# Heads stage of a hybrid decoder trunk: one more place for finished and for unfinished units, weights of a group in two transfers, their splits spread, attention's first loads moved

## Chip, cores and metric

One core of a Trainium2 chip runs the whole program. Times are device microseconds (us) of one execution, lower is better. The engines are called PE (TensorE; PEld is its weight load), DVE (VectorE), ACT (ScalarE), POOL (GpSimd) and SP (SyncE, here only the issuer of transfers).

## What is computed

Two decoder layers on 1024 tokens of width 1024 in float32. Layer 0 is a pooling and a short-convolution mixer, layer 1 is multi-head latent attention with 16 heads. The change lies in layer 1, between its input projection and its attention:

```python
q = (rms_norm(c_q, q_lat_g) @ w_uq).reshape(B, S, MLA_HEADS, QK_HEAD)
kv = (rms_norm(c_kv, kv_lat_g) @ w_ukv).reshape(B, S, MLA_HEADS, QK_NOPE + V_HEAD)
k_nope, v = kv[..., :QK_NOPE], kv[..., QK_NOPE:]
k = jnp.concatenate(
    [k_nope, jnp.broadcast_to(k_rope[:, :, None, :], (B, S, MLA_HEADS, QK_ROPE))], axis=-1)
q = rope_tail(rms_norm(q, q_head_g), cos, sin)
k = rope_tail(rms_norm(k, k_head_g), cos, sin)
o = causal_attention(q, k, v)
```

The latents have 768 (query) and 256 (key-value) columns, a head 64 plain and 32 rotated columns, and 64 columns of values.

## The kernel before

`front` computes layer 0 and the latents of layer 1 (up to 567 us of the span), `heads_and_attention` the heads and the attention, `final_projection` the rest. The change is in `heads_and_attention`, and in `Joint`, which holds what the first two share.

**Units.** The heads stage works on 32 units: 4 groups of 4 heads (g), each over 8 tiles of 128 tokens (t); u = 8 g + t. For exactness each float32 product is three matmuls, high x high, high x low, low x high (`three_passes`, L104 to L108), so each operand exists as a high half, rounded by ACT, and a low half, the rest, subtracted by DVE. A unit is on PE two chunks of the key-value weights (6 matmuls of 512 columns) and then six of the query weights (18 of 384).

**The way of a unit.** After PE, in step u:
- ACT copies v to its place (four places, `VSLOTS`), k and q to a place of `x` (seven, `XSLOTS`, L1340, L1346), and squares them (L1343, L1347).
- DVE sums the squares (L1448, L1452). After every fourth unit it takes the inverse roots for those four in a chain of 12 small operations (`root`, L1381 to L94). Then it scales unit u - 3 (L1405, L1406).
- POOL finishes a scaled unit: rotation and gain (`finish`, L1141 to L1506), and raises `turned`.
- ACT writes the high half of unit u - 5 to a place of `y` (two places, `head_split`, L1303). It waits for `turned` and for the store of the unit that had the place before, u - 7.
- DVE subtracts for the low half (L1410), and SP stores the place to `qk_scratch` in memory (L1236).

A step's waits and work stand in this order on each engine, and an engine does nothing past a wait that isn't met. PE may run about two units ahead: unit u needs the squares of unit u - 2, which need DVE's sums of unit u - 4.

**Weights of the next group.** While a group runs, the next one's weights are loaded (SP, `load_group`, at its first unit, for groups 2 and 3), and split by ACT (high, L1294) and DVE (low, L1375) in steps t = 3 to 6, by the table `when`. PE waits in the first unit of a group for each chunk (`w_done`). The raw weights of even and odd groups have one place each; even low halves lie where their raw ones were.

**Into attention.** SP reads keys and queries of a head back transposed (`load_k`, L1240, and `load_q`, L1243), and values of two heads at once (`load_v`, L1246). Their places (`k_t`, `q_t`) lie on space that the heads stage has left. The last units are finished inside attention: from unit 28 on by POOL alone, and their stores stand among attention's loads. In step 31 PE first computes the scores of the first two tiles of head 0, then unit 31. In attention, step n computes scores of tile n + 2, so head 1 (tile 8) is first used in step 6.

```python
            act.wait_ge(turned, w + 1)
            if w >= 2:
                act.wait_ge(y_stored[w % 2], 16 * (w // 2))
...
            if t == 0 and 1 <= g < G - 1:
                load_group(g + 1)
...
            store_v(u)
            if split_in(u) >= 0:
                store_qk(split_in(u))
```

SP has one queue, in program order: `load_group`, `store_v(u)`, `store_qk(u - 5)`, and, in some steps, the loads for attention ahead of them.

Of the kernel before, what the change touches and what calls it, by code (L numbers as in the profile page):

```python
# [142 lines left out]
class Joint:  # L143


    def __init__(self, nc, ctx, ring_at, w_place, lat_lo):
# [17 lines left out]
        self.kv_lo0, self.uq_lo0 = [kv_lo[:, k, :] for k in range(KKV)], [uq_lo[:, k, :] for k in range(KQ)]  # L164
        kv_hi = at("kv_hi0", [P, KKV, KVG], F32R, ring_at + tile)
# [843 lines left out]
def heads_and_attention(nc, w_ukv, w_uq, arena2, ring_at, w_place, banks_ps, joint, rms_qkv, rms_v, q_tab, k_rope, k_rope_ss,  # L1009
# [5 lines left out]
    XSLOTS, VSLOTS, LAG = 7, 4, 2  # L1015
# [24 lines left out]
    x = after("x", [P, XSLOTS, 2, HPG, QKH])  # L1040
    y = after("y", [P, 2, 2, HPG, BLK], F16)
# [18 lines left out]
    k_t = [at("k_t0", [P, 2, S], F16, ring_at), at("k_t1", [P, 2, S], F16, ring_at + TILE)]  # L1060
    q_t = [at("q_t0", [P, 2, S], F16, ring_at + 3 * TILE), at("q_t1", [P, 2, S], F16, ring_at + 2 * TILE)]
# [16 lines left out]
    w_landed = sem("w_landed")  # L1078
# [6 lines left out]
    y_stored = [sem(f"y_stored{e}") for e in range(2)]  # L1085
# [29 lines left out]
    when = {3: chunks[0:1], 4: chunks[1:3], 5: chunks[3:5], 6: chunks[5:8]}  # L1115
# [94 lines left out]
    def sync(sp):  # L1210
        def load_group(g):
# [17 lines left out]
        def store_qk(w):  # L1229
# [25 lines left out]
        for u in range(UNITS):  # L1255
# [35 lines left out]
    def scalar(act):  # L1291
        def weight_high(g, chunk):
            act.wait_ge(w_landed, 16 * NCH * g)
# [36 lines left out]
        for u in range(UNITS):  # L1330
# [9 lines left out]
            nc.scalar.activation(x[:, u % XSLOTS, 1, :, :NOPE], kv_view(u)[:, :, :NOPE], ACT.Copy, scale=rms_kv)  # L1340
# [5 lines left out]
            nc.scalar.activation(x[:, u % XSLOTS, 0], q_view(u), ACT.Copy, scale=rms_q)  # L1346
# [23 lines left out]
    def vector(dve):  # L1370
# [32 lines left out]
        def scale(w):  # L1403
            q, k = x[:, w % XSLOTS, 0], x[:, w % XSLOTS, 1, :, :NOPE]
# [359 lines left out]
```

## Time and profile before

| | us |
|---|---|
| median of 3 runs | 1048.66 (1046.89 to 1048.79) |
| the profiled execution, its own time | 1049.41 |
| span of its profile | 1047.4 |
| PE busy | 1017.0 (97%) |
| DVE busy | 616.3 (59%) |
| ACT busy | 465.0 (44%) |
| POOL busy | 211.1 (20%) |
| mean granted clock of PE over the span | 0.989 of full |

The profile is of one execution. Start times count from the span's start; a row of the timeline gives start, duration, engine, line of the kernel, operation, out<-in, shapes, and in brackets how long the engine was idle before it and what ended that. A wait for several things is put down to the one whose last event came last by the profile; where the engine named had long been done, it was another, often a transfer. A busy share is a mean over stages: the heads stage runs from 567 to 722 us, attention follows.

### The profile page before, as it was taken

How to read it: one execution, taken by the hardware profiler on the slowest of the kernel's cores; microseconds unless marked ns; L12 is line 12 of the kernel's file. 1: busy time of each engine (PE TensorE's matmuls, PEld its weight loads, DVE VectorE, ACT ScalarE, POOL GpSimd, SP SyncE). 2: the span in 40 equal slices, each digit the busy share in tenths (PEclk: the TensorE clock that was granted, in tenths of full speed). 3: DMA queues.
4: the chain of work that ended last, by engine and by line, in shares of the span. 5: the costliest groups of instructions: out<-in, count | busy, mean ns of one | idle time of the engine just before them, and what ended most of it. 6: DMA issues, size and time to landing. Idle time of an engine off the chain costs nothing. (4 is left out here: it accounts for less than half of the span.)

```text
span 1047.4 us, 15498 instructions
## 1 busy us (share of the span) xinstructions
PE 1017.0 (97%) x5979; PEld 846.2 (81%) x5979; DVE 616.3 (59%) x1111; ACT 465.0 (44%) x868; POOL 211.1 (20%) x301
## 2 busy tenths in 40 slices
PE   6999999999999999999999999999999999997998
PEld 4888888888888888888888998987777777775887
DVE  5653554445644543311344679798999999996221
ACT  6301111111132322322144657667999999997000
POOL 0000000000000001200001366786663332321000
PEclk9999999999999999999899999999999999998999
DMA  9300211211333431412112053664686564521221
GB/s 281 51 25 21 61 41 41 61 41 41 121 100 128 154 141 41 126 41 54 28 41 76 26 202 114 220 201 145 134 203 155 120 138 108 95 42 61 101 91 70
DMA packets 166425, 103.10 MB, mean 98 GB/s; under 512 B 76496, under 2 KB 150736, under 8 KB 166096
## 3 DMA queue, kind: packets, MB, share of 16 engines
q1 hardware_dynamic: 159280, 101.73, 34.4%
q10 hardware_dynamic: 7072, 0.39, 0.5%
q8 instruction: 47, 0.77, 0.3%
q14 instruction: 26, 0.21, 0.1%
HBM read 55.96 MB, written 29.36 MB: 81 GB/s over the span
## 5 line engine op out<-in xcount | busy, mean ns | idle before, releaser
L106 PE MATMUL banks<-front_act_hi,front_w_hi 128*128 128x512 f32 x608 | 240.8, 396 | 10.0 <-DVE front_w_lo L525 10.0
L107 PE MATMUL banks<-front_act_lo,front_w_hi 128*128 128x512 f32 x608 | 238.5, 392 | 0.0
L108 PE MATMUL banks<-front_act_hi,front_w_lo 128*128 128x512 f32 x608 | 238.5, 392 | 0.0
L106 PEld LDWEIGHTS banks<-front_act_hi,front_w_hi 128*128 128x128 f32 x608 | 115.4, 190 | 35.8 <-issue 8.5
L107 PEld LDWEIGHTS banks<-front_act_lo,front_w_hi 128*128 128x128 f32 x608 | 115.6, 190 | 24.4 <-issue 0.5
L108 PEld LDWEIGHTS banks<-front_act_hi,front_w_lo 128*128 128x128 f32 x608 | 115.3, 190 | 24.3
L392 ACT ACTIVATE front_w_hi<-front_w 128x1024 fp32r<-128x1024 f32 x43 | 45.6, 1060 | 147.2 <-DMA front_w<-in_w_in_ab 102.8
L1427 DVE TENSOR_TENSOR heads_pt_lo<-banks,heads_pt_hi 128x512 f16<-128x512 f32 (+2 forms) x192 | 102.1, 554 | 11.3 <-ACT heads_pt_hi L1318 6.7
L374 POOL TENSOR_TENSOR front_sq<-front_sq,front_squares 128x1024 f32<-128x1024 f32 x6 | 14.4, 2396 | 450.3 <-ACT front_squares L487 450.3
L1318 ACT ACTIVATE heads_pt_hi<-banks 128x512 f16<-128x512 f32 (+2 forms) x192 | 88.7, 486 | 10.3 <-PE banks L1586 10.2
L529 DVE TENSOR_TENSOR front_w_lo<-front_w,front_w_hi 128x1024 fp32r<-128x1024 f32 x43 | 52.3, 1219 | 42.8 <-ACT front_w_hi L392 42.6
L1604 PE MATMUL banks<-heads_v,heads_pt_hi 128*128 128x128 f16 x576 | 74.4, 220 | 0.9 <-DVE heads_pt_lo L1427 0.9
L1419 DVE CUSTOM_DVE_ANT_0 heads_probs_big<-banks,heads_mask,score_scale 128x1024 f32<-128x1024 f32 (+1 forms) x64 | 68.7, 1073 | 3.6 <-PE banks L108 2.6
L1586 PE MATMUL banks<-ident,heads_probs_big 128*128 128x128 f32 x416 | 69.0, 279 | 1.4 <-ACT heads_probs_big L1309 1.3
L1605 PE MATMUL banks<-heads_v,heads_pt_lo 128*128 128x64 f16 x576 | 69.4, 193 | 0.0
L1309 ACT ACTIVATE heads_probs_big<-heads_probs_big,heads_neg_max 128x1024 f32<-128x1024 f32 (+1 forms) x64 | 63.4, 991 | 5.5 <-DVE heads_neg_max L1419 3.3
L106 PE MATMUL banks<-heads_k_t,heads_q_t 96*128 96x512 f16 (+2 forms) x192 | 62.9, 328 | 1.8 <-DVE heads_neg_max L1419 1.8
L107 PE MATMUL banks<-heads_k_t,heads_q_t 96*128 96x512 f16 (+2 forms) x192 | 62.3, 324 | 0.0
L108 PE MATMUL banks<-heads_k_t,heads_q_t 96*128 96x512 f16 (+2 forms) x192 | 61.5, 325 | 0.0
L1604 PEld LDWEIGHTS banks<-heads_v,heads_pt_hi 128*128 128x128 f16 x576 | 54.0, 99 | 2.2 <-DVE heads_pt_lo L1427 1.0
L106 PE MATMUL out_proj<-gate_hi,w_out_hi 128*128 128x512 f32 x128 | 51.0, 398 | 2.7 <-DVE w_out_lo L961 2.6
L1605 PEld LDWEIGHTS banks<-heads_v,heads_pt_lo 128*128 128x128 f16 x576 | 51.3, 98 | 2.2
(246 smaller groups left out, 2067.7 us busy)
## 6 DMA issues: line engine op xcount, KB each, us to landing
qk_scratch<-heads_y SPq DMA_DIRECT2D x32, 512.0 KB, 3.7
front_w<-in_w_in_ab SPq DMA_DIRECT2D x21, 512.0 KB, 3.9
front_w<-in_w_in_c SPq DMA_DIRECT2D x17, 512.0 KB, 4.0
y<-in_x_t SPq DMA_DIRECT2D x8, 512.0 KB, 8.1
front_w<-in_w_out_ab SPq DMA_DIRECT2D x8, 512.0 KB, 3.8
front_x<-in_x_t SPq DMA_DIRECT2D x8, 512.0 KB, 5.1
x_scratch<-front_x SPq DMA_DIRECT2D x8, 512.0 KB, 4.0
v_scratch<-heads_v SPq DMA_DIRECT2D x32, 128.0 KB, 3.0
```

The source lines that it names most:

```text
L106: nc.tensor.matmul(out, w_hi, a_hi, start=first, stop=False)
L107: nc.tensor.matmul(out, w_hi, a_lo, start=False, stop=False)
L108: return nc.tensor.matmul(out, w_lo, a_hi, start=False, stop=last)
L392: nc.scalar.activation(weight(n, 1), weight(n, 0), ACT.Copy).then_inc(hi_done, 1)
L529: nc.vector.tensor_tensor(weight(n, 2), weight(n, 0), f32(weight(n, 1)), ALU.subtract).then_inc(lo_done, 1)
L1309: nc.scalar.activation(row, row, ACT.Exp, bias=neg_max[:, h % 2, i:i + 1], scale=-1.0, accum_out=total[:, h % 2, i:i + 1]).then_inc(exp_do ...
L1318: nc.scalar.activation(pt_hi[:, q % PIECES, :width], t_ps[:, banks[("piece", n, k)] % 3, :width], ACT.Copy).then_inc(pt_high, 1)
L1419: nc.vector.tensor_tensor_reduce(probs(n, 0, width), scores(i, 0, width), mask[:, S - width:], score_scale[:], 3e38, ALU.add, ALU.min, neg ...
L1427: nc.vector.tensor_tensor(pt_lo[:, q % PIECES, :width], t_ps[:, banks[("piece", n, k)] % 3, :width], pt_hi[:, q % PIECES, :width], ALU.sub ...
L1586: last = nc.tensor.transpose(t_ps[:, b, r * P:(r + 1) * P], probs(n, j * P, (j + 1) * P), ident[:])
L1604: nc.tensor.matmul(out, pt_hi[:, q % PIECES, blk], v2[e][:, j, :], start=(j == 0), stop=False)
L1605: last = nc.tensor.matmul(out[:, :VH], pt_lo[:, q % PIECES, blk], v2[e][:, j, :VH], start=False, stop=(j == i))
```

## The change

- `y` gets a third place and `x` an eighth. The new ones, `last_x` and `last_y`, lie on space of the first stage's weight ring. ACT's high half of unit w now waits for the store of unit w - 3.
- So the places of keys and queries move: `k_t0` and `q_t0` lie on the high weights of even groups, free when unit 23 is done; `k_t1` on their low query weights, free then too; `q_t1` on the high key-value weights of odd groups, free only when unit 31 is done on PE. Their loads move to later steps.
- `load_group` issues one transfer for the key-value weights and one for the query weights instead of two and six, with a semaphore for each.
- The table `when` spreads the eight splits over t = 2, 4, 5 and 6, two each.
- POOL clears `last_y` too.

```diff
@@ Joint @@
+        self.kv_raw_tile, self.uq_raw_tile = kv_raw, uq_raw
@@ heads_and_attention @@
-    XSLOTS, VSLOTS, LAG = 7, 4, 2
+    XSLOTS, YSLOTS, VSLOTS, LAG = 8, 3, 4, 2
...
-    x = after("x", [P, XSLOTS, 2, HPG, QKH])
-    y = after("y", [P, 2, 2, HPG, BLK], F16)
+    x, y = after("x", [P, XSLOTS - 1, 2, HPG, QKH]), after("y", [P, YSLOTS - 1, 2, HPG, BLK], F16)
+    last_x, last_y = at("last_x", [P, 2, HPG, QKH], F32, ring_at), at("last_y", [P, 2, HPG, BLK], F16, ring_at + 3 * TILE)
...
-    k_t = [at("k_t0", [P, 2, S], F16, ring_at), at("k_t1", [P, 2, S], F16, ring_at + TILE)]
-    q_t = [at("q_t0", [P, 2, S], F16, ring_at + 3 * TILE), at("q_t1", [P, 2, S], F16, ring_at + 2 * TILE)]
+    k_t = [at("k_t0", [P, 2, S], F16, ring_at + TILE), at("k_t1", [P, 2, S], F16, w_place + 2 * TILE)]
+    q_t = [at("q_t0", [P, 2, S], F16, ring_at + 2 * TILE), at("q_t1", [P, 2, S], F16, arena2)]
...
-    w_landed = sem("w_landed")
+    kv_landed, uq_landed = sem("kv_landed"), sem("uq_landed")
...
-    y_stored = [sem(f"y_stored{e}") for e in range(2)]
+    y_stored = [sem(f"y_stored{e}") for e in range(YSLOTS)]
...
-    when = {3: chunks[0:1], 4: chunks[1:3], 5: chunks[3:5], 6: chunks[5:8]}
+    when = {2: chunks[0:2], 4: chunks[2:4], 5: chunks[4:6], 6: chunks[6:8]}
...
+    def x_slot(w):
+
+        return last_x[:] if w % XSLOTS == XSLOTS - 1 else x[:, w % XSLOTS]
+
+    def y_slot(w):
+
+        return last_y[:] if w % YSLOTS == YSLOTS - 1 else y[:, w % YSLOTS]
...
@@ sync: load_group @@
-            for k in range(KKV):
-                sp.dma_start(kv_raw[g % 2][k], w_ukv[k * P:(k + 1) * P, g * KVG:(g + 1) * KVG]
-                             ).then_inc(w_landed, 16)
-            for k in range(KQ):
-                sp.dma_start(uq_raw[g % 2][k], w_uq[k * P:(k + 1) * P, g * QG:(g + 1) * QG]
-                             ).then_inc(w_landed, 16)
+            kv_tile, uq_tile = (kv_raw1, uq_raw1) if g % 2 else (joint.kv_raw_tile, joint.uq_raw_tile)
+            sp.dma_start(kv_tile[:], w_ukv.rearrange("(k p) c -> p k c", p=P)[:, :, g * KVG:(g + 1) * KVG]
+                         ).then_inc(kv_landed, 16)
+            sp.dma_start(uq_tile[:], w_uq.rearrange("(k p) c -> p k c", p=P)[:, :, g * QG:(g + 1) * QG]
+                         ).then_inc(uq_landed, 16)
...
@@ sync: the loop over units @@
-            if g == G - 2 and t == 4:
+            if g == G - 1 and t == 1:
                 group_stored(0)
+                sp.wait_ge(q_ready, (G - 1) * NT)
                 load_k(0)
-            if g == G - 2 and t == 6:
+            if g == G - 1 and t == 2:
                 load_q(0)
-            if g == G - 1 and t == 1:
-                sp.wait_ge(q_ready, (G - 1) * NT)
+            if g == G - 1 and t == 4:
                 load_k(1)
-            if g == G - 1 and t == 3:
-                load_q(1)
-            if g == G - 1 and t == 5:
+            if g == G - 1 and t == 6:
                 load_v(0)
             store_v(u)
+            if u == UNITS - 1:
+                sp.wait_ge(q_ready, UNITS)
+                load_q(1)
             if split_in(u) >= 0:
                 store_qk(split_in(u))
...
@@ scalar @@
-            act.wait_ge(w_landed, 16 * NCH * g)
+            act.wait_ge(kv_landed if chunk[0] == "kv" else uq_landed, 16 * g)
...
-            if w >= 2:
-                act.wait_ge(y_stored[w % 2], 16 * (w // 2))
+            if w >= YSLOTS:
+                act.wait_ge(y_stored[w % YSLOTS], 16 * (w // YSLOTS))
             else:
                 act.wait_ge(cleared, 1)
-            nc.scalar.activation(y[:, w % 2, :, :, :QKH], x[:, w % XSLOTS], ACT.Copy).then_inc(y_high, 1)
+            nc.scalar.activation(y_slot(w)[:, :, :, :QKH], x_slot(w), ACT.Copy).then_inc(y_high, 1)
...
@@ gpsimd @@
+        nc.gpsimd.memset(last_y[:].bitcast(F32), 0.0)
         nc.gpsimd.memset(y[:].bitcast(F32), 0.0).then_inc(cleared, 1)
```

Everywhere else `x[:, w % XSLOTS]` becomes `x_slot(w)` and `y[:, w % 2]` becomes `y_slot(w)`.

The order of instructions shows it at three places. The first is SP's queue at the start of group 2, where the third store of a unit stands ahead of the weights (`joint_kv_raw`, `joint_uq_raw`: the even group's raw weights). Before:

```order
L1236 DMA qk_scratch<-heads_y 256x1x1024
L1217 DMA joint_kv_raw_54<-in_w_ukv 128x512 x2
L1220 DMA joint_uq_raw_55<-in_w_uq 128x384 x6
L1226 DMA v_scratch<-heads_v 128x256
L1236 DMA qk_scratch<-heads_y 256x1x1024
```

and now:

```order
L1245 DMA qk_scratch<-heads_last_y 256x1x1024
L1227 DMA joint_kv_raw_54<-in_w_ukv 128x2x512
L1229 DMA joint_uq_raw_55<-in_w_uq 128x6x384
L1235 DMA v_scratch<-heads_v 128x256
L1245 DMA qk_scratch<-heads_y 256x1x1024
```

The eight issues between the stores of units 2 and 3 have become two.

The second is DVE in step 14, the last with splits of group 2's weights: sums, scaling, splits, low half of unit 9. Before:

```order
L1448 TENSOR_REDUCE heads_ss<-heads_sq 128x4
L1452 TENSOR_REDUCE heads_ss<-heads_sq 128x4
L1405 TENSOR_TENSOR heads_x<-heads_x,heads_rs 128x384
L1406 TENSOR_TENSOR heads_x<-heads_x,heads_rs 128x4x64
L1375 TENSOR_TENSOR joint_uq_lo_57<-joint_uq_raw_55,joint_uq_hi_1_60 128x384
L1375 TENSOR_TENSOR joint_uq_lo_57<-joint_uq_raw_55,joint_uq_hi_2_61 128x384 x2
L1410 TENSOR_TENSOR heads_y<-heads_x,heads_y 128x8x96
```

and now:

```order
L1458 TENSOR_REDUCE heads_ss<-heads_sq 128x4
L1462 TENSOR_REDUCE heads_ss<-heads_sq 128x4
L1415 TENSOR_TENSOR heads_x<-heads_x,heads_rs 128x384
L1416 TENSOR_TENSOR heads_x<-heads_x,heads_rs 128x4x64
L1385 TENSOR_TENSOR joint_uq_lo_57<-joint_uq_raw_55,joint_uq_hi_2_61 128x384 x2
L1420 TENSOR_TENSOR heads_y<-heads_x,heads_y 128x8x96
```

Two splits stand there instead of three; the first two of the group have moved from steps 11 and 12 to step 10.

The third is SP's queue at the end of the stage. Before, from the store ahead of step 27:

```order
L1236 DMA qk_scratch<-heads_y 256x1x1024
L1243 DMA_TRANSPOSE heads_q_t_125<-qk_scratch 128x2x1024
L1226 DMA v_scratch<-heads_v 128x256
L1236 DMA qk_scratch<-heads_y 256x1x1024
L1226 DMA v_scratch<-heads_v 128x256
```

and now, from the store of unit 25 ahead of step 31:

```order
L1245 DMA qk_scratch<-heads_y 256x1x1024
L1235 DMA v_scratch<-heads_v 128x256
L1252 DMA_TRANSPOSE heads_q_t_127<-qk_scratch 128x2x1024
L1245 DMA qk_scratch<-heads_last_y 256x1x1024
L1249 DMA_TRANSPOSE heads_k_t_124<-qk_scratch 128x2x1024
```

The queries of head 1 have moved from step 27 to behind everything but the store of unit 26; the keys of head 2 follow.

## Rows read from the trace of the kernel before

**Rows 1.** The page, part 1: busy time of the engines, share, instructions.
```profile
PE 1017.0 (97%) x5979; PEld 846.2 (81%) x5979; DVE 616.3 (59%) x1111; ACT 465.0 (44%) x868; POOL 211.1 (20%) x301
```

**Rows 2.** Timeline of PE: first matmuls of units and scores; start, duration.
```profile
567.43 0.39 PE L106 MATMUL banks<-joint_kv_hi,joint_lat_hi 128*128 128x512 f32 x1
...
639.88 0.39 PE L106 MATMUL banks<-joint_kv_hi,joint_lat_hi 128*128 128x512 f32 x1
...
644.90 0.55 PE L106 MATMUL banks<-joint_uq_hi,joint_lat_hi 128*128 128x384 f32 x1 [1.90 <-DVE joint_uq_lo L1375]
...
647.80 0.63 PE L106 MATMUL banks<-joint_kv_hi,joint_lat_hi 128*128 128x512 f32 x1
...
680.35 0.39 PE L106 MATMUL banks<-heads_kv_hi,joint_lat_hi 128*128 128x512 f32 x1
...
688.17 0.63 PE L106 MATMUL banks<-heads_kv_hi,joint_lat_hi 128*128 128x512 f32 x1
...
715.87 0.39 PE L106 MATMUL banks<-heads_k_t,heads_q_t 96*128 96x512 f16 x1
...
722.36 0.39 PE L106 MATMUL banks<-heads_k_t,heads_q_t 96*128 96x512 f16 x1
...
734.31 0.38 PE L106 MATMUL banks<-heads_k_t,heads_q_t 96*128 96x512 f16 x1 [0.69 <-DVE heads_neg_max L1419]
```

**Rows 3.** Windows, PE: stretch, length, busy, instructions, granted clock, DMA share, GB/s.
```profile
645.00:650.00 5.00, 5.00 (x18) 0.66 0.34 122
```

**Rows 4.** Timeline of DVE: first sums of units 8, 16, 24; waits; splits.
```profile
610.92 0.42 DVE L1448 TENSOR_REDUCE heads_ss<-heads_sq 128x4 f32<-128x256 f32 x1
...
625.10 0.96 DVE L1410 TENSOR_TENSOR heads_y<-heads_x,heads_y 128x768 f16<-128x768 f32 x1 [4.85 <-ACT heads_y L1303]
...
644.30 2.23 DVE L1375 TENSOR_TENSOR joint_uq_lo<-joint_uq_raw,joint_uq_hi 128x384 fp32r<-128x384 f32 x3
...
652.97 0.41 DVE L1448 TENSOR_REDUCE heads_ss<-heads_sq 128x4 f32<-128x256 f32 x1
...
665.57 1.20 DVE L1410 TENSOR_TENSOR heads_y<-heads_x,heads_y 128x768 f16<-128x768 f32 x1 [4.25 <-ACT heads_y L1303]
...
693.51 0.41 DVE L1448 TENSOR_REDUCE heads_ss<-heads_sq 128x4 f32<-128x256 f32 x1
```

**Rows 5.** Timeline of ACT: high half of unit 5.
```profile
624.22 0.84 ACT L1303 ACTIVATE heads_y<-heads_x 128x768 f16<-128x768 f32 x1 [5.90 <-POOLq L1507]
```

**Rows 6.** Timeline of POOL: last operation on unit 5.
```profile
617.87 0.46 POOL L1506 TENSOR_TENSOR heads_x<-heads_prod 128x128 f32<-128x128 f32 x1
```

**Rows 7.** Timeline of SP's queue: issues, start and duration.
```profile
611.66 1.48 SPq L1217 DMA_DIRECT2D joint_kv_raw<-in_w_ukv  x2
613.19 2.86 SPq L1220 DMA_DIRECT2D joint_uq_raw<-in_w_uq  x6
...
616.83 0.66 SPq L1236 DMA_DIRECT2D qk_scratch<-heads_y  x1
...
704.15 3.79 SPq L1243 DMA_TRANSPOSE heads_q_t<-qk_scratch  x1
...
724.67 0.72 SPq L1226 DMA_DIRECT2D v_scratch<-heads_v  x1
```

**Rows 8.** Issues from 616.5 to 617.4: count, KB, us to landing.
```profile
qk_scratch<-heads_y SPq DMA_DIRECT2D x1, 512.0 KB, 7.3
```

**Rows 9.** Issues from 611.5 to 616.05: the store of unit 2 among them.
```profile
joint_uq_raw<-in_w_uq SPq DMA_DIRECT2D x6, 192.0 KB, 4.8
qk_scratch<-heads_y SPq DMA_DIRECT2D x1, 512.0 KB, 3.7
```

**Rows 10.** Issues from 658.4 to 659: the store of unit 11.
```profile
qk_scratch<-heads_y SPq DMA_DIRECT2D x1, 512.0 KB, 5.9
```

**Rows 11.** The tile heads_y: durations in ns, least, median, most; first and last start.
```profile
L1410 DVE TENSOR_TENSOR heads_y<-heads_x,heads_y x27: 949/1211/1498, 599.0 to 730.8; 128x768 f16<-128x768 f32 x27
```

**Rows 12.** View of the transfers: all loads of a head's queries, median to landing.
```profile
heads_q_t<-qk_scratch SPq DMA_TRANSPOSE x16, 5.1
```

More of the change, by code:

```diff
@@ L1059, in heads_and_attention @@
     uq_lo = [joint.uq_lo0, chunks_of(at("uq_lo1", [P, KQ, QG], F32R, kv_at1 + half), KQ)]
-    k_t = [at("k_t0", [P, 2, S], F16, ring_at), at("k_t1", [P, 2, S], F16, ring_at + TILE)]
-    q_t = [at("q_t0", [P, 2, S], F16, ring_at + 3 * TILE), at("q_t1", [P, 2, S], F16, ring_at + 2 * TILE)]
+    k_t = [at("k_t0", [P, 2, S], F16, ring_at + TILE), at("k_t1", [P, 2, S], F16, w_place + 2 * TILE)]
+    q_t = [at("q_t0", [P, 2, S], F16, ring_at + 2 * TILE), at("q_t1", [P, 2, S], F16, arena2)]
+    assert 3 * TILE <= GROUP_W * 4
     probs_big0 = at("probs_big0", [P, S], F32, ring_at + 4 * TILE)
@@ L1138, in roots @@
         return rs[:, b % 2, j, which].unsqueeze(2)
+    def x_slot(w):
+        return last_x[:] if w % XSLOTS == XSLOTS - 1 else x[:, w % XSLOTS]
+    def y_slot(w):
+        return last_y[:] if w % YSLOTS == YSLOTS - 1 else y[:, w % YSLOTS]
     def k_turned(eng, w):
-        eng.tensor_tensor(x[:, w % XSLOTS, 1, :, NOPE:], k_rope[:, w % NT, :].unsqueeze(1).to_broadcast([P, HPG, ROPE]),
+        eng.tensor_tensor(x_slot(w)[:, 1, :, NOPE:], k_rope[:, w % NT, :].unsqueeze(1).to_broadcast([P, HPG, ROPE]),
                           roots(w, 1).to_broadcast([P, HPG, ROPE]), ALU.mult)
     def times_gain(eng, w):
-        nope = x[:, w % XSLOTS, 0, :, :NOPE]
+        nope = x_slot(w)[:, 0, :, :NOPE]
         eng.tensor_tensor(nope, nope, gain[:].unsqueeze(1).to_broadcast([P, HPG, NOPE]), ALU.mult)
@@ L1236, in store_qk @@
             sp.dma_start(qk_d[t * P:(t + 1) * P, :, g * HPG * BLK:(g + 1) * HPG * BLK],
-                         y[:, w % 2].rearrange("p q h d -> p q (h d)")).then_inc(y_stored[w % 2], 16)
+                         y_slot(w).rearrange("p q h d -> p q (h d)")).then_inc(y_stored[w % YSLOTS], 16)
         def load_k(h):
@@ L1248, in group_stored @@
         def group_stored(g):
-            for e in range(2):
-                sp.wait_ge(y_stored[e], 16 * (NT // 2) * (g + 1))
+            for e in range(YSLOTS):
+                sp.wait_ge(y_stored[e], 16 * len(range(e, NT * (g + 1), YSLOTS)))
             for e in range(VSLOTS):
@@ L1339, in scalar @@
                 act.wait_ge(y_low, u - XSLOTS + 1)
-            nc.scalar.activation(x[:, u % XSLOTS, 1, :, :NOPE], kv_view(u)[:, :, :NOPE], ACT.Copy, scale=rms_kv)
+            nc.scalar.activation(x_slot(u)[:, 1, :, :NOPE], kv_view(u)[:, :, :NOPE], ACT.Copy, scale=rms_kv)
             if u >= 2:
@@ L1345, in scalar @@
             act.wait_ge(q_ready, u + 1)
-            nc.scalar.activation(x[:, u % XSLOTS, 0], q_view(u), ACT.Copy, scale=rms_q)
+            nc.scalar.activation(x_slot(u)[:, 0], q_view(u), ACT.Copy, scale=rms_q)
             nc.scalar.activation(q_squares(u), q_view(u), ACT.Square, scale=rms_q).then_inc(q_squared, 1)
@@ L1403, in scale @@
         def scale(w):
-            q, k = x[:, w % XSLOTS, 0], x[:, w % XSLOTS, 1, :, :NOPE]
+            q, k = x_slot(w)[:, 0], x_slot(w)[:, 1, :, :NOPE]
             nc.vector.tensor_tensor(q, q, roots(w, 0).to_broadcast([P, HPG, QKH]), ALU.mult)
@@ L1409, in head_split @@
             dve.wait_ge(y_high, w + 1)
-            nc.vector.tensor_tensor(y[:, w % 2, :, :, P:P + QKH], x[:, w % XSLOTS], y[:, w % 2, :, :, :QKH],
+            nc.vector.tensor_tensor(y_slot(w)[:, :, :, P:P + QKH], x_slot(w), y_slot(w)[:, :, :, :QKH],
                                     ALU.subtract).then_inc(y_low, 1)
@@ L1488, in finish @@
             t = w % NT
-            q, k = x[:, w % XSLOTS, 0], x[:, w % XSLOTS, 1, :, :NOPE]
+            q, k = x_slot(w)[:, 0], x_slot(w)[:, 1, :, :NOPE]
             if w < LATE:
@@ L1510, in late_low @@
             pool.wait_ge(y_high, w + 1)
-            nc.gpsimd.tensor_tensor(y[:, w % 2, :, :, P:P + QKH], x[:, w % XSLOTS], y[:, w % 2, :, :, :QKH],
+            nc.gpsimd.tensor_tensor(y_slot(w)[:, :, :, P:P + QKH], x_slot(w), y_slot(w)[:, :, :, :QKH],
                                     ALU.subtract).then_inc(y_low_late, 1)
```

## The prediction

> **What bounds the kernel now.** I read the page first for the share of each engine, then TensorE (PE) in order of time through the heads stage, then the granted clock of that stretch, then the engine that TensorE waited for, and from there back until a transfer stood at the end. PE is busy for 97% of the span [rows 1], so time can only come out of its few gaps. The reader should see in [rows 2] that PE paces the heads stage: unit 0 starts at 567.43, unit 16 at 639.88, so a unit takes 72.45 / 16 = 4.53 us. Unit 16 then takes 7.92 (to 647.80) and unit 24 takes 7.82 (680.35 to 688.17). In unit 16 PE stood still for 1.90 us until VectorE (DVE) had made a low part of the next group's query weights (L1375). It then ran slow: the granted clock of 645 to 650 is 0.66 of full [rows 3], a mean of the two levels 1.2 and 2.4 GHz, after a stretch in which PE had been idle. The 7 units 17 to 23 take 32.55 where 7 x 4.53 = 31.71 was due, units 25 to 30 take 27.70 where 27.18 was due.
>
> So the two stalls cost 7.92 - 4.53 = 3.39, 7.82 - 4.53 = 3.29, and behind them 0.84 and 0.52: **8.0 us**. All of it lies on the path that sets the end: attention starts only when PE has done unit 31, and PE is the pace there too.
>
> **Why DVE was late.** In unit 14 three splits ran from 644.30 for 2.23 us [rows 4]. The first of them was due when three of six query chunks were used up. A unit is 6 matmuls of 512 columns and 18 of 384, so a query chunk (3 x 384) is 0.52 us and the two key-value chunks are 1.4: due at 639.88 + 1.4 + 1.56 = 642.8. DVE was late because it had stood 4.85 us before the low half of unit 5 (to 625.10), and 4.25 us before that of unit 13 (to 665.57) [rows 4]. Both times it waited for ScalarE (ACT), which started unit 5's high half at 624.22 after 5.90 idle [rows 5]. That row names POOL, but POOL had ended unit 5 at 617.87 + 0.46 = 618.33 [rows 6]. What ended the wait was the place: unit 5 takes the place of unit 3, whose store was issued at 616.83 [rows 7] and landed 7.3 us later [rows 8], at 624.13. The store had been ready since the low half of unit 3, but stood in SP's queue behind eight weight loads from 611.66 to 616.05 [rows 7], and its bytes behind theirs. The store before it, of unit 2, landed in 3.7 [rows 9]. The store of unit 11, behind the next group's loads, took 5.9 [rows 10] and held up unit 13 in the same way.
>
> **The change, part by part.**
>
> *Three places for finished units.* Unit 5 now waits for the store of unit 2 (issued before the loads of 611.66 and landed 3.7 us later [rows 9], by 615.4), so ACT can take it when POOL has finished it, at 618.33, 5.8 us earlier. Unit 6 needs the store of unit 3, unit 7 that of unit 4, each one turn later than before. Unit 13 needs the store of unit 10 instead of 11. This removes the 4.85 and the 4.25 from DVE's path.
>
> *Two loads for eight.* SP gives eight issues of 1.48 + 2.86 us in all [rows 7] for two. I take some 0.5 us for each (the single issue at 616.83 took 0.66), so the store of unit 3 goes out up to 3 us sooner; the bytes are the same. ACT asks for the key-value part two units earlier than DVE used it before (now in unit 10, at about 618, before in unit 11). The last of the eight loads was issued by 616.05 and landed 4.8 later [rows 9], so nothing lands after 620.9 even at the old pace: the wait is between 0 and 2.9 us. I take 0, because the key-value part goes first and its separate semaphore does not wait for the query part.
>
> *Splits spread.* The eight splits cost DVE the same. None is left in the unit with the root chain (t = 3), and the last unit carries two instead of three. Cost 0; the last one simply comes as late as the group's work ends.
>
> *Eight places for unfinished units.* Unit u now takes the place of unit u - 8 instead of u - 7, so ACT waits for an older low half. Before, ACT met this wait only while DVE was already behind; worth 0 on the path once DVE is on time, and I count no gain for it. The extra memset on POOL comes before unit 0, whose result POOL and ACT need only after the first root chain, four units later: covered.
>
> *What is late next: DVE's own work.* Group 1 (units 8 to 15) begins on DVE at 610.92 and group 2 at 652.97: 42.05, less 4.85 is 37.2. Group 2 to group 3 (693.51) is 40.54, less 4.25 is 36.3 [rows 4]. PE needs 36.2 for a group. So DVE is only just fast enough. Group 2 would begin at 610.92 + 37.2 = 648.1, and the last split ends 6.4 us before that (652.97 - 646.5), at 641.7; PE needs it at 639.88 + 4.53 - 0.52 = 643.9. Margin 2.2. For the next group: last split 648.1 + 36.3 - 6.4 = 678.0, needed at 676.1 + 4.0 = 680.1. Margin 2.1. Both stalls go.
>
> *Against it: DVE beside POOL.* The subtraction of L1410 takes 0.949 at least, 1.211 in the median and 1.498 at most, always for the same shape [rows 11]. While DVE stood 4.85 and 4.25 us POOL worked alone; that POOL work now falls beside DVE work. Bounds for what it adds: 0, if the slow cases were already in the 37.2, and 4.85 x (1.498 / 0.949 - 1) = 2.8 for the first group, 2.5 more for the second. I take 0.7 each: the median ratio 1.28, on about half of DVE's time, since the root chain and the reductions are small or read one input. The margins become 1.5 and 0.7, still above 0. By the upper end the second is -3.2 and part of a stall returns. The Trainium skill, SBUF - State Buffer, section "Who interferes with whom", says that a DVE instruction with two SBUF inputs and a GpSimd instruction that reads SBUF exclude each other, the second one blocked until the first is done. By that rule the overlap that is added is paid in full, and the sum would go by the upper end, with part of the second stall back (rival A); the trace agrees that there is a block, with the spread of one shape from 0.949 to 1.498, and does not show how much of it is new.
>
> *Loads for attention moved.* The keys and queries of head 0 go from units 20 and 22 to 25 and 26, head 1's keys from 25 to 28, values from 29 to 30, and head 1's queries from 27 to behind unit 31. Head 0 is first used at 715.87 [rows 2]; SP was at unit 27 by 704.15 [rows 7], 11.7 us before, and a transpose lands 5.1 after its issue [rows 12]: cost 0, cover over 6 us. Head 1 is first used at 734.31 [rows 2], 11.95 after attention starts at 722.36. Its last load now stands behind the store of v at 724.67 + 0.72 [rows 7], so it goes out at 725.4 and lands at 730.5. Cost 0, cover 3.8 us; without that cover each us late is a us of PE. Nothing else waits behind it but the store of unit 26, due later.
>
> **Sum.** 1049.41 (the profiled execution; its span is 1047.4) - 8.0 = 1041.4. The median of the runs shown is 0.75 lower, which would give 1040.7. I forecast 1041.0. About 0.2%, 2.1 us, is what a measurement of this kernel can tell from no change.
>
> **Rivals.**
>
> A, *one stall half returns.* DVE's work, not the wait, is the limit in group 2: margins of 2 us on 36 are thin, and L1410 takes up to 1.498 beside POOL [rows 11]. Against: the 37.2 of group 1 still holds shorter waits. (The rule of the SBUF page speaks for this rival.) Price: 0.5 to 3.8 (a stall of 3.29 with its tail 0.52), time 1041.5 to 1045.2. Decides from a stretch of 2.1 us over the two groups.
>
> B, *the change doesn't do what it says.* ACT, taken off the store, waits as long for POOL (`turned`) or for a weight load at the head of its queue. For it: the row at 624.22 names POOL. Against: POOL had ended 5.9 us earlier. Both stalls stay: 1048 to 1049.
>
> C, *slower.* If DVE's two-input work were stretched everywhere by the median ratio 1.28, a group would take 36.3 x 1.28 = 46.5, 10 more than PE. Two groups make 20, less the 2.1 of margin: PE loses 18 where it lost 8, time about 1059. It turns into a loss from 8.0 + 2.1 = 10 us of stretch on 73.5, 14%. Against: POOL ran beside DVE for most of the stage already, and only 9 us of 83 were apart.
>
> D, *head 1's queries late.* The landing would have to slip by more than 3.8 us from the median. Price up to 3: 1041 to 1044.
>
> **How the numbers follow.** Forecast 0.62, A 0.22, B 0.08, C 0.04, D 0.04. Faster by over 0.2%: forecast, A and D, less a little for luck, 0.86; within: B and that little, 0.10; slower 0.04. The range takes the forecast and A and leaves out B and C. Below, the runs of before spread by 1.9 us, and 1040.7 - 1.9 is about 1039.0. Above, rival A ends at 1045.2; 1045.5.
>
> **What would show it.** Right: PE unit starts of 4.53 apart from 0 to 30, no fall of the granted clock between 640 and 690, attention starting near 714.4; ACT's idle before the high halves of units 5 and 13 under 1 us; DVE's first reduction of unit 16 near 649. Wrong: a wait of PE for L1385 in unit 24 (A), idle of ACT before unit 5 with the store landed (B), L1420 with a median above 1.4 us (C), or a PE wait some 12 us into attention that ends with the load of head 1's queries (D). If PE's stalls go and the time falls by less than 6 us, the gain was given back in attention.

## The result, and the profile after

The changed kernel takes **1040.7 us** (median of 4 runs, 1039.96 to 1041.57) against 1048.1 for the kernel before on the same chip (4 runs, 1046.89 to 1048.79): a ratio of 0.9931 with the interval [0.9914, 0.9948]. The forecast was 1041.0 in a range of 1039.0 to 1045.5. The profiled execution took 1039.96, the shortest of its four runs; its span is 1037.9.

The page of the changed kernel, part 1, answers to [rows 1]:

```profile
PE 1012.6 (98%) x5979; PEld 844.0 (81%) x5979; DVE 618.8 (60%) x1111; ACT 464.2 (45%) x868; POOL 211.9 (20%) x302
```

The timeline of PE, changed kernel, answers to [rows 2]: the first matmuls of units 0, 16 and 24, then of the first scores, of attention and of head 1.

```profile
567.33 0.39 PE L106 MATMUL banks<-joint_kv_hi,joint_lat_hi 128*128 128x512 f32 x1
...
639.54 0.39 PE L106 MATMUL banks<-joint_kv_hi,joint_lat_hi 128*128 128x512 f32 x1
...
675.64 0.39 PE L106 MATMUL banks<-heads_kv_hi,joint_lat_hi 128*128 128x512 f32 x1
...
707.24 0.39 PE L106 MATMUL banks<-heads_k_t,heads_q_t 96*128 96x512 f16 x1
...
713.73 0.39 PE L106 MATMUL banks<-heads_k_t,heads_q_t 96*128 96x512 f16 x1
...
726.05 0.38 PE L106 MATMUL banks<-heads_k_t,heads_q_t 96*128 96x512 f16 x1 [0.70 <-DVE heads_neg_max L1429]
```

Sixteen units take 72.21, eight more 36.10: 4.51 us each, without a stall. Attention starts at 713.73 where it started at 722.36, 8.63 sooner, of which 0.10 was there at unit 0. Its end keeps the lead: the final projection starts at 945.76, before at 954.40, 8.64 sooner.

Windows of PE, changed kernel (stretch, length, busy and matmuls, granted clock, DMA share, GB/s); the first answers to [rows 3]:

```profile
645.00:650.00 5.00, 5.00 (x28) 1.00 0.22 80
725.00:730.00 5.00, 4.30 (x31) 0.68 1.06 249
```

Full speed where 0.66 was granted before. The second row is a surprise that I come back to.

The timeline of DVE, changed kernel, answers to [rows 4]: first sums of units 8, 16 and 24, and the last splits of the two groups.

```profile
610.04 0.41 DVE L1458 TENSOR_REDUCE heads_ss<-heads_sq 128x4 f32<-128x256 f32 x1
...
639.81 1.22 DVE L1385 TENSOR_TENSOR joint_uq_lo<-joint_uq_raw,joint_uq_hi 128x384 fp32r<-128x384 f32 x2
...
648.06 0.41 DVE L1458 TENSOR_REDUCE heads_ss<-heads_sq 128x4 f32<-128x256 f32 x1
...
677.10 1.22 DVE L1385 TENSOR_TENSOR heads_uq_lo<-heads_uq_raw,heads_uq_hi 128x384 fp32r<-128x384 f32 x2
...
685.43 0.41 DVE L1458 TENSOR_REDUCE heads_ss<-heads_sq 128x4 f32<-128x256 f32 x1
```

The groups take 38.02 and 37.37. The last splits end at 641.03 and 678.32.

ACT's high half of unit 5, changed kernel, answers to [rows 5], and the weight part that ACT splits ahead of it:

```profile
618.11 1.15 ACT L1304 ACTIVATE joint_kv_hi<-joint_kv_raw 128x512 fp32r<-128x512 f32 x2
619.15 0.84 ACT L1313 ACTIVATE heads_last_y<-heads_x 128x768 f16<-128x768 f32 x1
```

No bracket stands behind either: ACT waited for neither a store nor a load. The high half of unit 13 (655.54) has no bracket either. SP's queue at the start of group 2, and in attention the issue of head 1's queries, answer to [rows 7]:

```profile
610.79 0.61 SPq L1227 DMA_DIRECT2D joint_kv_raw<-in_w_ukv  x1
611.44 0.87 SPq L1229 DMA_DIRECT2D joint_uq_raw<-in_w_uq  x1
...
613.30 0.80 SPq L1245 DMA_DIRECT2D qk_scratch<-heads_y  x1
...
716.70 2.49 SPq L1252 DMA_TRANSPOSE heads_q_t<-qk_scratch  x1
```

Landings of these issues, changed kernel (count, KB, us from issue to landing); the last answers to [rows 8]:

```profile
joint_uq_raw<-in_w_uq SPq DMA_DIRECT2D x1, 1152.0 KB, 9.0
...
joint_kv_raw<-in_w_ukv SPq DMA_DIRECT2D x1, 512.0 KB, 6.5
...
qk_scratch<-heads_y SPq DMA_DIRECT2D x1, 512.0 KB, 8.7
```

The store of unit 3 goes out 3.5 us sooner (613.30, before 616.83), takes 8.7 for 7.3, and lands at 622.0, 2.1 sooner. Of the 3.5, 0.9 is that the loads ahead of it were issued that much sooner (610.79, before 611.66). The key-value weights land at 617.3, 0.8 before ACT asks.

### The profile page after: what moved, and what is told of

Read it like the earlier page. It is cut to its first block and busy times, and to the rows that moved or that the text cites. A ratio compares the mean times of both kernels' runs of the same rounds, so it can differ in the third digit from the quotient of the medians.

```text
span 1037.9 us, 15485 instructions
## 1 busy us (share of the span) xinstructions
PE 1012.6 (98%) x5979; PEld 844.0 (81%) x5979; DVE 618.8 (60%) x1111; ACT 464.2 (45%) x868; POOL 211.9 (20%) x302
## 5 line engine op out<-in xcount | busy, mean ns | idle before, releaser
L1429 DVE CUSTOM_DVE_ANT_0 heads_probs_big<-banks,heads_mask,score_scale 128x1024 f32<-128x1024 f32 (+1 forms) x64 | 68.6, 1072 | 3.6 <-PE banks L108 2.6
```

Source lines behind the costliest of these rows:

```text
L1429: nc.vector.tensor_tensor_reduce(probs(n, 0, width), scores(i, 0, width), mask[:, S - width:], score_scale[:], 3e38, ALU.add, ALU.min, neg ...
```

## The experiments

Each is the changed kernel with an edit; `...` marks lines left out of a diff. What was measured is the median (range, number of runs), and the ratio to the kernel before from runs on the same chip. Those of before had medians of 1047.45 to 1048.57. Line numbers shift a little where an edit adds lines.

### Which part carries the gain

**Two places for finished units** (`e1_two_y`), all else as changed.

```diff
-    XSLOTS, YSLOTS, VSLOTS, LAG = 8, 3, 4, 2
+    XSLOTS, YSLOTS, VSLOTS, LAG = 8, 2, 4, 2
```

> The changed kernel with two places for finished units (y) instead of three, all else as changed. If the third place is what took the stalls away: unit 5 waits for the store of unit 3 again, which in the changed kernel's trace is issued at 613.3 and lands at 622.0, while POOL is done at 618; ACT idle about 3 us there and about 3.5 before unit 13, more than DVE's margins (2.5 us at unit 16, 1.3 at unit 24), so both PE stalls come back, smaller than before because the store goes out earlier: 1042 to 1046 us. If the two transfers or the spread splits did it: 1040.7, as changed.

Measured: 1044.11 (1041.34 to 1045.84, 6), ratio 0.9960 [0.9945, 0.9975]. Timeline of ACT, then of PE, in this run:

```profile
620.56 0.84 ACT L1313 ACTIVATE heads_last_y<-heads_x 128x768 f16<-128x768 f32 x1 [2.57 <-DMA qk_scratch<-heads_last_y]
...
659.75 0.85 ACT L1313 ACTIVATE heads_last_y<-heads_x 128x768 f16<-128x768 f32 x1 [3.57 <-DMA qk_scratch<-heads_last_y]
...
708.72 0.84 ACT L1313 ACTIVATE heads_y<-heads_x 128x768 f16<-128x768 f32 x1 [1.80 <-DMA qk_scratch<-heads_y]
```

```profile
661.75 0.50 PE L106 MATMUL banks<-joint_kv_hi,joint_lat_hi 128*128 128x512 f32 x1 [0.75 <-ACT heads_sq L1353]
...
679.62 0.45 PE L106 MATMUL banks<-heads_uq_hi,joint_lat_hi 128*128 128x384 f32 x1 [0.56 <-DVE heads_uq_lo L1385]
...
719.76 0.66 PE L1597 MATMUL banks<-ident,heads_probs_small 128*128 128x128 f32 x4 [1.88 <-ACT heads_sq L1357]
```

The store's wait is back, and now named as a transfer. But the time returned only by half, and elsewhere than I had put it. Unit 16 has no stall; PE waits 0.75 for ACT's squares before unit 21 and 0.56 for a split in unit 24, and from unit 0 to unit 31 it takes 2.1 longer than in the changed kernel. The largest single wait, 1.88, is in attention, where ACT still has squares of the last unit to do: it had stood for stores four more times between 693 and 709, the last time before 708.72. The high half at 708.72 starts 2.98 later than its like in the changed kernel (705.74), DVE's first maximum of scores (L1429) follows 3.28 later (713.68 for 710.40), and ACT's squares with it, for which PE stands the 1.88. The third place thus does two things, and I had seen one. The kernel before has two places too, but other loads in the queue there, and no such wait in attention: it seems that the second thing makes good what the moved loads would cost. Not all of the 1.88 need come from stores, for four of the runs below with three places (`e2_y_alone`, `e4_eight_loads`, `e5_old_when`, `e6_again_one`) wait 0.45 to 0.98 for the same squares. And against the kernel before, this run gains 3.8: with two places, the other parts are worth something.

**The third place alone** (`e2_y_alone`): seven places of `x`, eight loads with one semaphore, the old `when`. The places of keys and queries and attention's loads stay as changed, since the third place needs their room.

```diff
-    XSLOTS, YSLOTS, VSLOTS, LAG = 8, 3, 4, 2
+    XSLOTS, YSLOTS, VSLOTS, LAG = 7, 3, 4, 2
...
-    when = {2: chunks[0:2], 4: chunks[2:4], 5: chunks[4:6], 6: chunks[6:8]}
+    when = {3: chunks[0:1], 4: chunks[1:3], 5: chunks[3:5], 6: chunks[5:8]}
...
-            act.wait_ge(kv_landed if chunk[0] == "kv" else uq_landed, 16 * g)
+            act.wait_ge(w_landed, 16 * NCH * g)
```

> The third place for finished units alone (with the moved places and loads that it needs); seven places of x, eight loads, the old table of splits. If the third place is what matters: no stall of PE in units 16 and 24, 1041 us; the store of unit 3 goes out late, at about 616.8, and holds up unit 6 by 1 to 1.5 us, inside DVE's margin of 2.5. If the transfers or the spreading carry a share: a stall in unit 16 or 24 remains, 1043 to 1046 us.

Measured: 1041.17 (1039.71 to 1042.38, 6), ratio 0.9934 [0.9921, 0.9948]. That is the whole gain, within what can be told. PE's only wait for a split in this run is short, and in unit 24:

```profile
680.69 0.45 PE L106 MATMUL banks<-heads_uq_hi,joint_lat_hi 128*128 128x384 f32 x1 [0.23 <-DVE heads_uq_lo L1386]
```

**The parts costed at 0**, each undone by itself: seven places of `x` (`e3_seven_x`), eight loads (`e4_eight_loads`), the old table (`e5_old_when`). Their diffs are the first, third and second pieces above; with the third go the eight load instructions of the kernel before.

> The changed kernel with seven places of x instead of eight. By the sum the eighth is worth nothing on the path: 1040.7 us, no stall. Rival: with DVE some 4 us behind PE, ACT now meets the wait for an older low half, falls behind, and a stall returns: 1042 or more.

> The changed kernel with the eight weight loads and their one semaphore, the splits spread as changed. ACT then waits in unit 10 until the last load lands (issued about 615, landed 620, while it asks at 618.1): 2 us of idle, inside the margin of 2.5 at unit 16; at unit 24 the same 2 us are more than the margin of 1.3: 1040.7 to 1042 us. Rival, that the number of transfers decides the whole: both stalls back, 1046 to 1048.

> The changed kernel with the old table of splits (3, 4, 5, 6 with 1, 2, 2, 3). DVE's work in a group is the same, so its last split ends at the same time: 1040.7 us. Only if the three splits at the end run into the first chunks' due times (three are due 1.0 us before the last) does a short stall return: at most 1 us.

| | median | range, runs | ratio |
|---|---|---|---|
| seven `x` | 1040.74 | 1039.49 to 1042.61, 5 | 0.9925 [0.9913, 0.9937] |
| eight loads | 1040.66 | 1039.82 to 1042.97, 5 | 0.9930 [0.9918, 0.9942] |
| old table | 1042.13 | 1041.73 to 1042.5, 5 | 0.9938 [0.9925, 0.9952] |

The first two are worth nothing that can be measured. Eight loads do make ACT wait in the new table's order, 2.06 for group 2's weights and 3.22 for group 3's, and PE loses a little of the second (ACT in group 2, then PE in unit 24):

```profile
620.84 1.16 ACT L1305 ACTIVATE joint_kv_hi<-joint_kv_raw 128x512 fp32r<-128x512 f32 x2 [2.06 <-DMA joint_uq_raw<-in_w_uq]
```

```profile
680.17 0.44 PE L106 MATMUL banks<-heads_uq_hi,joint_lat_hi 128*128 128x384 f32 x1 [0.32 <-DVE heads_uq_lo L1386]
```

ACT splits a key-value part there, but the row names the load of query weights that ended the wait. So the separate semaphore is what keeps that 2.06 away. PE loses 0.32 by it in this execution, and the median shows no loss. With the old table PE waits 0.22 in unit 24 and the median is 1.5 higher, but the two intervals overlap: whether the spread is worth a microsecond stays open.

### How thin DVE's margin is

**More work on DVE** (`e6_again_one`, `e7_again_three`): one low half, or three, of each group computed twice, in step 1, or in steps 1, 4 and 5, of groups 1 and 2. The diff is that of `e7_again_three`; in `e6_again_one` the tuple is `(1,)`. `w + 5` is the step in which unit w is split.

```diff
+    AGAIN = [u for u in range(8, 24) if u % 8 in (1, 4, 5)]
...
         def head_split(w):
             dve.wait_ge(y_high, w + 1)
+            if w + 5 in AGAIN:
+                link(nc.vector.tensor_tensor(y_slot(w)[:, :, :, P:P + QKH], x_slot(w), y_slot(w)[:, :, :, :QKH],
+                                             ALU.subtract))
```

> The changed kernel, with one low half (L1420, 1.2 us) computed twice by DVE in each of groups 1 and 2. If DVE's own work is the next bound, as the sum had it (margins now 2.5 us at unit 16 and 1.3 at unit 24): no stall at 16, a stall of about 1.2 at 24, 1042 to 1043 us. If DVE has more slack than I think: 1040.7.

> The changed kernel, with three low halves (3 x 1.25 us) computed twice by DVE in each of groups 1 and 2. If DVE is the next bound: 3.75 less 2.5 is a stall of 1.3 at unit 16 and, with the slow clock behind it, a stall of 2 to 3.5 at unit 24; 1044 to 1048 us. If there is more slack: 1041 to 1042.

Measured: one, 1040.20 (1039.36 to 1041.62, 6), ratio 0.9926 [0.9913, 0.9939]; three, 1045.58 (1043.46 to 1047.82, 12), ratio 0.9975 [0.9965, 0.9984]. One was a miss: nothing lost where I had expected 1042 to 1043. The last splits there, on DVE's timeline:

```profile
639.98 1.22 DVE L1386 TENSOR_TENSOR joint_uq_lo<-joint_uq_raw,joint_uq_hi 128x384 fp32r<-128x384 f32 x2
...
677.94 1.22 DVE L1386 TENSOR_TENSOR heads_uq_lo<-heads_uq_raw,heads_uq_hi 128x384 fp32r<-128x384 f32 x2
```

They start 0.17 and 0.84 later than in the changed kernel, for one and two extra operations of 1.21 and 1.22. In the changed kernel DVE has two waits for ACT in group 1, of 0.18 and 0.95; here the second is gone. The extra work took its place, and the sums of unit 16 start at 648.06 in both. Three were too many; PE, with the window around it:

```profile
682.30 0.63 PE L106 MATMUL banks<-heads_uq_hi,joint_lat_hi 128*128 128x384 f32 x1 [2.87 <-DVE heads_uq_lo L1386]
```

```profile
680.00:700.00 20.00, 17.70 (x85) 0.91 0.59 158
```

The stall is in unit 24, as rival A had it, with the slow clock behind it (0.91 over 20 us). The 1.3 us that I had expected in unit 16 did not come: PE has no wait there.

**More work on POOL, none on DVE** (`e9_pool_again`): the two products of the rotation computed twice in 12 of the 16 units of the two groups.

```diff
+    AGAIN = [u for u in range(8, 24) if u % 4 != 3]
...
             link(ins)
+            if w + 3 in AGAIN:
+                for a in range(2):
+                    ins = nc.gpsimd.tensor_tensor(
+                        prod[:, 2 * a:2 * a + 2], halves,
+                        q_tab[:, 2 * a:2 * a + 2, t, :].unsqueeze(2).to_broadcast([P, 2, HPG, HALF]), ALU.mult)
+                link(ins)
```

> The changed kernel, with POOL's two rotation products (L1511, about 0.65 us each) computed twice for 6 of 8 units of groups 1 and 2; DVE, ACT and PE do the same work as before. If POOL's work beside DVE's is what stretches DVE (my term of 0.7 us a group): DVE's time from its first sums of unit 8 to those of unit 24 grows though it has nothing more to do, by 1 to 4 us on 75.4, L1420's median rises above 1.21, POOL falls behind (5.3 us a unit where PE has 4.5) and ACT waits for it; a stall may return, 1041 to 1045 us. If the engines don't hinder each other and POOL has slack: 1040.7 and the same 75.4.

Measured: 1044.88 (1043.15 to 1047.04, 6), ratio 0.9966 [0.9952, 0.9979]. Busy time of POOL, then of DVE, from the first sums of unit 8 to those of unit 24, first in this run:

```profile
610.79:690.57 79.78, 69.54 (x105) 0.98 0.51 175
610.79:690.57 79.78, 76.45 (x146) 0.98 0.51 175
```

and in the changed kernel:

```profile
610.04:685.43 75.39, 58.35 (x81) 1.00 0.54 185
610.04:685.43 75.39, 71.96 (x146) 1.00 0.54 185
```

DVE's timeline in this run: first sums of units 8, 16 and 24, and the last splits of group 3's weights; then PE:

```profile
610.79 0.41 DVE L1459 TENSOR_REDUCE heads_ss<-heads_sq 128x4 f32<-128x256 f32 x1
...
651.33 0.41 DVE L1459 TENSOR_REDUCE heads_ss<-heads_sq 128x4 f32<-128x256 f32 x1
...
681.27 1.54 DVE L1386 TENSOR_TENSOR heads_uq_lo<-heads_uq_raw,heads_uq_hi 128x384 fp32r<-128x384 f32 x2
...
690.57 0.41 DVE L1459 TENSOR_REDUCE heads_ss<-heads_sq 128x4 f32<-128x256 f32 x1
```

```profile
682.13 0.44 PE L106 MATMUL banks<-heads_uq_hi,joint_lat_hi 128*128 128x384 f32 x1 [2.09 <-DVE heads_uq_lo L1386]
```

DVE got not one instruction more (146 in both), yet its groups take 40.54 and 39.24 for 38.02 and 37.37, 4.4 us more. POOL has 24 operations more and is busy 11.2 us longer: **0.39 us of DVE for each us of POOL**. The 4.4 is not waiting. DVE's busy time grew by 4.5 and its idle time did not (3.3, before 3.4), though ACT now waits 19 us for POOL where it waited 3.3. So POOL's work is paid on DVE, by operations that last longer: the root chains by 4.3 in all, the scaling by 0.8 and the splits by 0.5, while the low halves (L1420) took 1.1 less. PE stalls in unit 24.

The Trainium skill, SBUF - State Buffer, section "Who interferes with whom", has a vector operation with two inputs in SBUF contend with a GpSimd operation that reads SBUF. The trace agrees: the pair of splits, with two inputs, takes 1.54 for 1.22, and DVE's sums, with one input, keep their 0.41. If each excluded the other whenever both run, an added us of POOL would cost DVE up to 1 us; measured is 0.39.

### The cover of head 1's queries

**Head 1's queries one place later** (`e8_q1_late`): behind the store of unit 26.

```diff
+            if split_in(u) >= 0:
+                store_qk(split_in(u))
             if u == UNITS - 1:
                 sp.wait_ge(q_ready, UNITS)
                 load_q(1)
-            if split_in(u) >= 0:
-                store_qk(split_in(u))
```

> The changed kernel with the load of head 1's queries one place later in SP's queue, behind the store of unit 26 (issued at 723.6): it goes out at 724.2 and lands at 729, where PE wants it at 726.05. If the cover is what I worked out: PE waits about 3 us there, 1043 to 1045 us. If something else hides it (DVE is the pace in attention's first steps): under 1 us more, 1041 to 1041.5.

Measured: 1044.01 (1042.96 to 1045.93, 6), ratio 0.9963 [0.9950, 0.9976], 3.3 over the changed kernel. PE's first scores of head 1:

```profile
728.90 0.61 PE L106 MATMUL banks<-heads_k_t,heads_q_t 96*128 96x512 f16 x1 [4.82 <-DMA heads_q_t<-qk_scratch]
```

The store is issued at 722.31 here, and the transpose cannot leave before. In the changed kernel it leaves at 716.70 and lands 4.7 later, at 721.4, for a use at 726.05. The order in SP's queue is right and has 4.6 us to spare. The wait of 4.82 costs 3.3 in the median; part of it is a wait for DVE that PE has there in any case (0.70 in the changed kernel).

### Versions meant to be better

**Root chain later** (`e10_root_later`): the inverse roots of units 28 to 31, and the high halves of these units, come four steps of attention later. **Last splits later** (`e11_split_later`): both halves of unit 26 and the high half of unit 27 three steps later.

```diff
-    ROOT_STEP, LAST_SPLIT = 3, 2
+    ROOT_STEP, LAST_SPLIT = 7, 2
...
-        return 3 + NT * (w - LATE_LOW)
+        return 3 + NT * (w - LATE_LOW) + (4 if w > LATE_LOW else 0)
```

```diff
-    ROOT_STEP, LAST_SPLIT = 3, 2
+    ROOT_STEP, LAST_SPLIT = 3, 5
...
-        return 3 + NT * (w - LATE_LOW)
+        return 3 + NT * (w - LATE_LOW) + (3 if w == LATE_LOW else 0)
```

> The changed kernel with the last chain of roots in attention's steps 7 to 10 instead of 3 to 6 (and the high halves of units 28 to 31 four steps later). PE waits for DVE (L1429) three times in those steps, 0.5 to 0.7 us each. If that chain is what makes DVE late there: 0.5 to 2 us less, 1039 to 1040.2. If DVE's maxima and low parts set the pace whatever else it does: 1040.7, or more, if the wait only moves.

> The changed kernel with the halves of unit 26 in attention's step 5 instead of 2, and the high half of unit 27 in step 6 instead of 3. The low half is 0.96 us of DVE, after 0.76 us of waiting for ACT. If that is what makes DVE late in the first steps: up to 1 us less, 1039.7. If not: 1040.7; the store of unit 26 then holds up the loads of head 2 by some 3 us, which have more cover than that.

> The changed kernel itself once more, beside the two above on one chip: 1040 to 1042 us, ratio 0.993.

Measured: 1046.27 (1044.92 to 1048.51, 12), ratio 0.9986 [0.9976, 0.9996], for the root chain; 1040.57 (1039.99 to 1040.81, 5), ratio 0.9926 [0.9912, 0.9939], for the last splits; and 1039.98 (1039.68 to 1041.37, 5), ratio 0.9925 [0.9911, 0.9939], for the changed kernel run again beside them (`e12_changed_again`). The second edit moves nothing that can be measured. The first was a miss: 1039 to 1040.2 expected, 6.3 us over the changed kernel beside it. Its POOL, ACT and PE:

```profile
737.00 0.40 POOL L1151 TENSOR_TENSOR heads_x<-k_rope,heads_rs 128x128 f32<-128x128 f32 x1 [19.19 <-DVEq L1411]
...
745.21 0.72 POOL L1539 TENSOR_TENSOR heads_o_sum<-heads_o_raw 128x256 f32<-128x256 f32 x1 [0.18 <-POOL heads_x L1516]
```

```profile
746.02 0.69 ACT L1335 ACTIVATE heads_o_raw<-banks,v_unscale 128x512 f32<-128x512 f32 x1 [5.34 <-POOL heads_o_sum L1539]
```

```profile
748.64 1.09 PE L1597 MATMUL banks<-ident,heads_probs_big 128*128 128x128 f32 x4 [4.93 <-ACT heads_probs_big L1319]
```

POOL begins unit 28 when the roots are there, at 737.00 instead of 731.48, and works on two units before its first sum for attention (L1539), which slips from 739.69 to 745.21. ACT cannot write the next output until that sum has read the place, and PE stands 4.93 for ACT. An engine busy for 20% of the span had set the time. Of all versions none beats the changed kernel.

## Why the prediction was right

- **The two stalls** (8.0 = 3.39 + 3.29 + 0.84 + 0.52). Both went, with what followed them. PE gains 8.53 from unit 0 to the start of attention. The 0.5 over 8.0 comes from the size of a unit. The 4.53 is a mean over units 0 to 15; most of them took 4.51, and units 12 and 13, behind ACT's first long wait, 4.63 and 4.64. Against 4.51 every term is a little larger, and 0.24 more was lost in those two units. The tail of 0.84 is not all slow clock, as the prediction had it: unit 17 took 4.84, and behind ACT's second long wait units 20 and 21 took 5.02 and 4.63, with PE waiting for ACT's squares at full clock. PE's timeline, kernel before:

```profile
666.69 0.50 PE L106 MATMUL banks<-joint_kv_hi,joint_lat_hi 128*128 128x512 f32 x1 [0.34 <-ACT heads_sq L1343]
```

  The span fell by 9.5 (1047.4 to 1037.9); the 0.9 beyond 8.63 arises in the final projection, which the change doesn't touch. The medians differ by 7.4. The profile of before was one of its longer executions, as the 0.75 of the prediction took in, and that of the changed kernel the shortest of four, so the two traces show more than the medians.
- **The cause, a place held by its store.** ACT waited for no store any more; where a row still names POOL, it was POOL (its longest, 3.12, ends at 689.04, POOL's work at 688.95). `e1_two_y` brings the wait back under its true name, and `e2_y_alone` gains as much as the whole change. Rival B is out. What the prediction missed is the end of the stage: with two places and attention's moved loads in SP's queue, ACT waits for stores there as well, and PE's longest wait in `e1_two_y`, 1.88, comes at least in part from those. It also counted the parts one by one: the others are worth 0 beside the third place, but 3.8 without it.
- **Two loads, eight `x`, spread: 0.** Right for the first two (`e4_eight_loads`, `e3_seven_x`); for the third 0 to 1.5, open. ACT's wait for the load was to be 0 to 2.9, taken 0: it was 0, with 0.8 to spare. The step "the store of unit 3 goes out up to 3 us sooner" held for the issue (3.5, of which 2.7 is the shorter queue); of this 2.1 reached the landing.
- **DVE's margins** (1.5 and 0.7 after a term of 0.7 each for POOL beside it). Measured in the same way, the last splits end at 641.03 and 678.32 where 643.5 and 679.6 were due: 2.5 and 1.3. The group times, waits for ACT taken out, grew by 38.02 - 37.2 = 0.8 and 37.37 - 36.3 = 1.1. But DVE's other idle time shrank meanwhile, and its busy time shows the stretch by itself. Windows of DVE over the two groups, before and then changed:

```profile
610.92:652.97 42.05, 34.86 (x73) 0.96 0.48 166
652.97:693.51 40.54, 34.59 (x73) 0.96 0.62 198
```

```profile
610.04:648.06 38.02, 35.78 (x73) 1.00 0.54 184
648.06:685.43 37.37, 36.18 (x74) 1.00 0.54 187
```

  The stretch is 0.9 and 1.6, so the term of 0.7 was near for the first group and less than half for the second; its upper end (2.8 and 2.5) did not come. (That end was too high: in the two long waits POOL was busy for 3.6 and 3.9 us, not for all of 4.85 and 4.25.) Three things made up for it: DVE's idle time outside the long waits fell from 2.3 and 1.7 to 2.2 and 1.2, DVE began group 1 at 610.04 and not at 610.92, and the splits end 7.0 and 7.1 before the group's end, not 6.4 (648.06 - 641.03, 685.43 - 678.32). That the margins came out above the forecast is in part luck. Rival A and rival C are real mechanisms (`e7_again_three`, `e9_pool_again`), only too small here. My test for C, a median of L1420 above 1.4, was a bad one. In `e9_pool_again` that median stays at 1.21 while DVE loses 4.4 us: the stretch falls on the roots above all.
- **Head 1's queries**: cover 3.8 predicted, 4.6 in the trace, 3.3 us lost when it is taken away.
- **The sum**: 1041.0 against 1040.7. The stalls were 0.5 larger than counted and the gain of the medians 0.6 smaller than 8.0, so the nearness is partly luck; the mechanism is not.

## What to carry over

When an engine waits for two things and the profile names one that had long been done, look for a place in memory whose store is still under way, and count where that store stands in its queue. One more place was worth 7 us here, and fewer transfers and smoother splits nothing measurable beside it, though with two places all the other parts together gained 3.8: gains of parts that cure the same wait do not add up. A wait removed leaves the next bound close by: measure its distance by adding work to it (one operation a group cost nothing, three cost 5 us), also on an engine whose work stretches it.

## What was not expected of the hardware

- **A fall of the granted clock without a stall ahead of it.** Between 725 and 730 the changed kernel was granted 0.68 of full, a mean of 1.2 and 2.4 GHz; before it PE had only short idle times (0.35 at 718.55, 0.57 at 723.97, 0.38 at 724.69, 0.70 at 726.05). The kernel before has the same ones (0.36, 0.56, 0.38 and 0.69, the last at 734.31) and is granted 1.00 there. The fall cost attention nothing: the lead is 8.26 at head 1's first scores and 8.27 at 757.58, behind it. The kernel before waits 0.53 at 738.31 for DVE and 0.30 at 743.60 for ACT, and the changed one does not: the slower PE used time that it would have waited. I have no explanation of the fall from these traces.
- **Fewer transfers did not land sooner.** The 1152 KB of query weights in one transfer took 9.0, issued at 611.44 they landed at 620.4, 9.6 after the first issue of that group's weights. Before, the last two of the eight loads took 5.2, which puts the last landing at about 621, 9.5 after the first issue at 611.66. The store behind the two loads took 8.7 for 7.3. Fewer issues on SP saved SP's time; that the landing is bound by the bytes ahead fits this and was not tested.
- **A small operation on DVE can last until POOL's big one beside it ends.** The 128x32 TENSOR_SCALAR of the root chain (L1392) takes 0.18 at 643.80 in the changed kernel, with POOL idle, but 0.60 at 660.61, where it ends at 661.21 and POOL's operation at 661.18. In `e9_pool_again` one takes 0.60 and ends at 646.18, POOL's at 646.15. Of the six of these that lasted longer than 0.18 in the two traces, five end 0.03 or 0.04 behind an operation of POOL (between 600 and 690). DVE's row and POOL's, of `e9_pool_again`:

```profile
645.58 0.60 DVE L1393 TENSOR_SCALAR heads_ss<-heads_ss 128x32 f32<-128x32 f32 x1
```

```profile
645.39 0.76 POOL L1157 TENSOR_TENSOR heads_x<-heads_x,gain 128x256 f32<-128x256 f32 x1
```

For it the price was what was left of the other engine's operation, not a share of its own time. It has one input in SBUF. The section of the Trainium skill named above exempts one input only outside the modes that use both ports, and names `tensor_scalar` among the operations that can enter them; which mode this one ran in no row shows.
